# Hybrid attention on one Trainium2 core: scaling on GpSimd, outputs on ScalarE, and scores on the two row halves of the array

## The reference, cut to what matters

```
for each head h, branch b, tile t of 128 queries:
    s    = q[t, h] . k_b[keys up to the tile's end]^T / sqrt(64) + bias_b
    p    = exp(s - max s);   sum = p.sum() (+ exp(sink - max s) for "ban")
    fac  = 1 / sum, times gate_b[t, h] for the three branches of the first mixer
    y[t] += (p * fac) . v_b
```

## Time and profile before

| | us |
|---|---|
| median of 3 runs | 3504.17 (3500.81 to 3507.8) |
| the profiled execution, its own time | 3509.27 |
| its span in the profile | 3507.5 |
| busy in the span: PE, DVE, ACT, POOL | 2892.5, 1526.5, 452.8, 886.6 |
| mean granted TensorE clock | 0.903 of full |

### The profile page before, as it was taken

The page is one execution under the profiler, slowest core; times in us unless marked ns, Lnnn a source line. Parts: engine busy times, 40 slices in busy tenths (PEclk is TensorE's granted clock), DMA queues, the critical chain, the costliest instruction groups (busy, mean ns, idle before and its releaser), DMA issues.

```text
span 3507.5 us, 25672 instructions
## 1 busy us (share of the span) xinstructions
PE 2892.5 (82%) x9302; PEld 1717.2 (49%) x9302; DVE 1526.5 (44%) x2316; ACT 452.8 (13%) x1020; POOL 886.6 (25%) x633
## 2 busy tenths in 40 slices
PE   5999887989999999999997899477776666666666
PEld 3444656478888884444456647133332222222222
DVE  5664364122210000001016704765666667767765
ACT  1000232011011010001005501000010001100000
POOL 2111100000000000000000002554556566666663
PEclk9999878999999999999988999798897887888788
DMA  9999420356544443444640045999999999999998
GB/s 380 395 401 341 124 83 15 120 197 222 201 147 155 155 148 140 155 150 137 218 136 1 2 145 218 418 384 417 379 401 422 422 421 422 408 422 422 422 421 355
DMA packets 232373, 922.71 MB, mean 263 GB/s; under 512 B 17819, under 2 KB 37475, under 8 KB 160355
## 3 DMA queue, kind: packets, MB, share of 16 engines
q0 software_dynamic: 99840, 637.57, 44.3%
q1 hardware_dynamic: 132181, 283.96, 23.8%
q10 hardware_dynamic: 272, 0.13, 0.0%
HBM read 918.41 MB, written 8.44 MB: 264 GB/s over the span
## 4 chain that ended last, share of the span: by engine, by line
PE 55%; DMA 25%; DVE 11%; POOL 4%; issue 2%; ACT 2%; DVEq 0%; POOLq 0%; SPq 0%; ACTq 0%
PE ps L1219 17%; PE ps L907 11%; DMA arena<-in_peer_v,proj 10%; PE ps L1245 9%; PE ps L1444 6%; DMA proj<-in_peer_v,proj 4%; DMA proj<-in_peer_u,proj 4%; DMA ring<-in_w_in 3%; DMA arena<-in_w_mod 3%; PE ps L1028 3%; POOL arena L487 3%; PE ps L1421 2%; DVE proj L2049 1%; POOL proj L487 1%; DVE arena L2049 1%
## 5 line engine op out<-in xcount | busy, mean ns | idle before, releaser
L1444 PE MATMUL ps<-proj,gates 128*128 128x512 f32 x992 | 576.0, 745 | 394.2 <-DMA proj<-in_peer_v,proj 272.2
L1219 PE MATMUL ps<-hT,ring 128*128 128x256 f32 x2816 | 608.2, 379 | 1.5 <-ACT hT L526 1.5
L1444 PEld LDWEIGHTS ps<-proj,gates 128*128 128x128 f32 x992 | 233.3, 243 | 733.6 <-issue 604.3
L1219 PEld LDWEIGHTS ps<-hT,ring 128*128 128x128 f32 x2816 | 535.0, 190 | 74.9 <-issue 2.2
L487 POOL DMA_INDIRECT proj<-in_peer_u,proj x128 | 204.8, 1600 | 1427.6 <-DVE proj L2042 1265.1
L907 PE MATMUL ps<-ring,hT 128*128 128x512 f32 (+2 forms) x960 | 381.7, 558 | 8.7 <-DMA ring<-in_w_in 8.7
L2049 DVE CUSTOM_DVE_ANT_0 arena<-arena,yT 128x2048 f32<-128x2048 f32 x128 | 291.5, 2291 | 211.4 <-DMA arena<-in_peer_u,proj 210.9
L2049 DVE CUSTOM_DVE_ANT_0 proj<-proj,yT 128x2048 f32<-128x2048 f32 x128 | 292.1, 2291 | 126.8 <-DMA proj<-in_peer_u,proj 122.7
L1245 PE MATMUL ps<-ring,arena 128*128 128x512 f32 x704 | 304.1, 595 | 2.7 <-ACT arena L725 2.7
L907 PEld LDWEIGHTS ps<-ring,hT 128*128 128x128 f32 x960 | 175.6, 194 | 214.5 <-issue 192.6
L1444 PE MATMUL ps<-arena,gates 128*128 128x512 f32 x512 | 237.3, 607 | 35.9 <-DMA arena<-in_peer_v,proj 35.7
(11 more groups left out here) (410 smaller groups left out, 2568.3 us busy)
## 6 DMA issues: line engine op xcount, KB each, us to landing
arena<-in_w_mod POOLq DMA_DIRECT2D x96, 1024.0 KB, 12.4
ring<-in_w_in SPq DMA_DIRECT2D x52, 1024.0 KB, 12.1
ring<-in_ffn_w_gate SPq DMA_DIRECT2D x44, 1024.0 KB, 5.2
ring<-in_ffn_w_up SPq DMA_DIRECT2D x44, 1024.0 KB, 5.2
ring<-in_ffn_w_down SPq DMA_DIRECT2D x44, 1024.0 KB, 4.8
ring<-in_w_out SPq DMA_DIRECT2D x32, 1024.0 KB, 5.2
ring<-in_peer_wq SPq DMA_DIRECT2D x16, 1024.0 KB, 10.9
ring<-in_w_in SPq DMA_DIRECT2D x16, 960.0 KB, 18.2
```

The costliest lines, as they stand in the source:

```text
L1219: ins = pe.matmul(ps[:, 4 * m + f, 0:T], ring[:, s, k, P * f:P * (f + 1)], hT[:, KS * s + k, :], start=(s == 0 and k == 0), stop=(s == SLO ...
L1444: ins = pe.matmul(ps[:, 4 * t + b, :], diag[:, j, :], row_slots[n % ROWS][:, NB * b:NB * (b + 1)], start=(h == 0 and j == 0), stop=(h == H ...
```

## The change

What goes to which engine changes, and the order on PE:

- The multiplication of a unit by its factors goes from DVE to POOL (`scaled`). DVE signals `att_fac` when the factors are there; POOL waits for it and signals `att_p`. `q_in` goes to POOL too, behind `scaled(0)` of each pair, and the very first ahead of all pairs.
- `attended` goes from DVE to ACT, behind `turned_out(0)` and `turned_out(1)` of the next pair.
- `hyb["q"]` keeps both heads of a pair side by side in its two row halves, with two buffers that alternate by pair. It needs no zeros, so its memset goes, and `q_out` is two activations of 128 rows instead of four of 64.
- `score` is one head: a matmul of 64 rows, head 0 on the upper and head 1 on the lower row half. `half_scores(u, 0)` issues head 0 of unit u and head 1 of unit u + 1, `half_scores(u, 1)` the two others; between them PE waits until the first two have ended, as one bank would otherwise be written from both halves. PE does this at odd u only, for units u + 3 and u + 4, the first half ahead of `turn_p(u)` and the second behind it.
- All eight pairs are straight code on PE; ACT's loop takes two pairs a turn.

```diff
@@ GpSimd @@
+        def scaled(i, past, u):
+            t, br = UNITS[u]
+            n = {"cmp": (7, 15)[t]}.get(br, P * (t + 1))
+            pool_eng.wait_ge(*at("att_fac", at_unit(i, past, u + 1)))
+            p = hyb["p"][:, u % 4, :, 0:n]
+            pool_eng.tensor_tensor(p, p, hst["sum"][:, u, :].unsqueeze(2).to_broadcast([P, 2, n]), ALU.mult).then_inc(sem("att_p"), 1)
+        def head_pair(i, past, more=True):
+            for u in range(NU):
+                scaled(i, past, u)
+                if u == 0 and more:
+                    pool_eng.wait_ge(*(at("att_turned", at_unit(i, past, -3)) if past else at("q_turned", 1)))
+                    q_in(i, past + 1)
+        pool_eng.wait_ge(*at("kv_twice", 1))
+        q_in(0, 0)
...
@@ ScalarE @@
-        def q_out(k):
-            for h in range(2):
-                r = slice(DK * h, DK * (h + 1))
-                ins = act.activation(hyb["q"][r, k, h, :], ps[r, 4 + k, T:2 * T], ACT.Copy, scale=DK ** -0.5)
-            ins.then_inc(sem("q_out"), 1)
+        def q_out(pair, k):
+            act.activation(hyb["q"][:, pair % 2, k, :], ps[:, 4 + k, T:2 * T], ACT.Copy, scale=DK ** -0.5).then_inc(sem("q_out"), 1)
...
+        def attended(i, past, k, u):
+            act.wait_ge(*at("att_pv", at_unit(i, past, u + 2)))
+            act.copy(yT[:, bass.ds(i + (past + 8 * k), 1), :], ps[:, 6 + k, 0:T].unsqueeze(1)).then_inc(sem("att_out"), 1)
...
                 turned_out(i, past, u, more)
+                if u < 2 and past:
+                    attended(i, past - 1, u, NU - 2 + u)
...
@@ TensorE @@
-        def score(i, past, u):
+        def score(i, past, u, h, second):
...
+            r = slice(DK * h, DK * (h + 1))
+            ins = pe.matmul(ps[:, u % 4, T * h:T * h + n], hyb["q"][r, (past + u // NU) % 2, int(br == "ban"), P * t:P * (t + 1)], keys[r], start=True, stop=True)
+            if second:
+                ins.then_inc(sem("att_score"), 1)
+            return ins
+        def half_scores(i, past, u, n):
+            for v, h in (((u, 0), (u + 1, 1)), ((u, 1), (u + 1, 0)))[n]:
+                ins = score(i, past, v, h, n)
+            return ins
...
             for u in range(NU):
-                if u + 4 < NU or more:
-                    score(i, past, u + 4)
+                ahead = u % 2 and (u + 3 < NU or more)
+                if ahead:
+                    half_scores(i, past, u + 3, 0).then_inc(sem("first_half"), 1)
                 turn_p(i, past, u, more)
+                if ahead:
+                    pe.wait_ge(*at("first_half", i * 4 + (4 * past + u // 2 + 3)))
+                    half_scores(i, past, u + 3, 1)
                 if u:
                     values(i, past, u - 1)
...
@@ VectorE @@
-        link(vec.memset(hyb["q"], 0.0), "q_zero")
...
-                link(vec.tensor_tensor(s, s, gate, ALU.mult))
-            p = hyb["p"][:, u % 4, :, 0:n]
-            link(vec.tensor_tensor(p, p, s.unsqueeze(2).to_broadcast([P, 2, n]), ALU.mult), "att_p", wait=False)
+                link(vec.reciprocal(s, s))
+                link(vec.tensor_tensor(s, s, gate, ALU.mult), "att_fac", wait=False)
...
                 weigh(i, past, u)
                 if u + 3 < NU or more:
                     row_max(i, past, u + 3)
-                if u == 0 and more:
-                    vec.wait_ge(*(at("att_turned", at_unit(i, past, -3)) if past else at("q_turned", 1)))
-                    q_in(i, past + 1)
-                if u == 1 and past:
-                    attended(i, past - 1, 1, NU - 1)
-            attended(i, past, 0, NU - 2)
```

More of the change, by code:

```diff
@@ L483, in _, with q_in @@
                 pool_eng.dma_start(mod["late"][:, j % 4], w_mod[:, 2 * j:2 * j + 2, (10 + n) * MB:(11 + n) * MB]).then_inc(sem(f"mod_slot{j % 4}"), 16)
+        def q_in(i, past):
+            for k, col in enumerate((QA, QB)):
+                ins = pool_eng.tensor_copy(hyb["q_in"][:, k], p2[:, :, bass.ds(i * P + (col + P * past), P)])
+            ins.then_inc(sem("q_in"), 1)
+        def scaled(i, past, u):
[12 more added lines that the diff above has]
+        q_in(0, 0)
+        head_pair(0, 0)
+        with pool_eng.Fori(0, 6) as i:
+            head_pair(i, 1)
+        head_pair(0, 7, False)
         def gather(table, g, r, n):
@@ L770, in turned_out @@
             if more and u in (2, 3):
-                q_out(u - 2)
+                q_out(past + 1, u - 2)
             if past or u >= 2:
@@ L775, in turned_out @@
             act.copy(hyb["pT"][0:r, u % 2, 0:n, :], ps[0:r, 4 + u % 2, 0:P * n].rearrange("p (a b) -> p a b", b=P)).then_inc(sem("att_pT"), 1)
-        act.wait_ge(*at("q_zero", 1))
         act.wait_ge(*at("q_turned", 1))
         for k in range(2):
-            q_out(k)
+            q_out(0, k)
         for u in range(2):
             softmax_exp(0, 0, u)
+        def attended(i, past, k, u):
+            act.wait_ge(*at("att_pv", at_unit(i, past, u + 2)))
+            act.copy(yT[:, bass.ds(i + (past + 8 * k), 1), :], ps[:, 6 + k, 0:T].unsqueeze(1)).then_inc(sem("att_out"), 1)
         def head_pair(i, past, more=True):
@@ L789, in head_pair @@
                 turned_out(i, past, u, more)
+                if u < 2 and past:
+                    attended(i, past - 1, u, NU - 2 + u)
         head_pair(0, 0)
-        with act.Fori(0, 6) as i:
+        with act.Fori(0, 6, 2) as i:
             head_pair(i, 1)
+            head_pair(i, 2)
         head_pair(0, 7, False)
+        for k in range(2):
+            attended(0, 7, k, NU - 2 + k)
         act.wait_ge(*at("att_out", 17))
@@ L1287, in _ @@
         pe.wait_ge(*at("kv_out", 1))
-        def score(i, past, u):
+        def score(i, past, u, h, second):
             t, br = UNITS[u % NU]
             g = kv_head(past, u)
-            if past or u >= 4:
+            if not second and (past or u >= 4):
                 pe.wait_ge(*at("att_exp", at_unit(i, past, u - 2)))
-            if u in (NU, NU + 3):
+            if not second and u in (NU, NU + 3):
                 pe.wait_ge(*at("q_out", i * 2 + (2 * past + 3 + u // (NU + 3))))
[L1297 to L1306, removed]
+            if br == "cmp":
+                n = (7, 15)[t]
+                keys = hyb["kc"][:, g, 0:n]
+            else:
+                n = P * (t + 1)
+                keys = hyb["kT"][:, 2 * ("slc", "win", "ban").index(br) + g, 0:n]
+            r = slice(DK * h, DK * (h + 1))
[7 more added lines that the diff above has]
+            return ins
         def turn_q(k):
@@ L1366, in _ @@
         pe.wait_ge(*at("q_out", 2))
[L1367 to L1376, removed]
+        for u in (0, 2):
+            half_scores(0, 0, u, 0).then_inc(sem("first_half"), 1)
+            pe.wait_ge(*at("first_half", u // 2 + 1))
+            half_scores(0, 0, u, 1)
+        for pair in range(8):
+            head_pair(0, pair, pair < 7)
         values(0, 7, NU - 1)
@@ L1892, in _ @@
             vec.memset(stat[:, 17 + k:18 + k], 0.0).then_inc(sem(name), 1)
-        link.n["att_out"] = 1
         vec.wait_ge(*at("evac_act", EVB["out2"] + 2))
@@ L1901, in _ @@
         vec.memset(hyb["v"], 0.0)
-        vec.memset(hyb["v_cmp"], 0.0)
-        link(vec.memset(hyb["q"], 0.0), "q_zero")
+        link(vec.memset(hyb["v_cmp"], 0.0))
         for kind in range(3):
@@ L1947, in weigh @@
             t, br = UNITS[u]
-            n = {"cmp": (7, 15)[t]}.get(br, P * (t + 1))
             vec.wait_ge(*at("att_exp", at_unit(i, past, u + 2)))
@@ L1952, in weigh @@
                 link(vec.tensor_tensor(s, s, hst["esink"][:, u, :], ALU.add))
-            link(vec.reciprocal(s, s))
-            if br != "ban":
+                link(vec.reciprocal(s, s), "att_fac", wait=False)
+            else:
                 gate = hst["gate"][:, 3 * t + ("cmp", "slc", "win").index(br), bass.ds(i * 2 + 2 * past, 2)]
-                link(vec.tensor_tensor(s, s, gate, ALU.mult))
-            p = hyb["p"][:, u % 4, :, 0:n]
-            link(vec.tensor_tensor(p, p, s.unsqueeze(2).to_broadcast([P, 2, n]), ALU.mult), "att_p", wait=False)
+                link(vec.reciprocal(s, s))
+                link(vec.tensor_tensor(s, s, gate, ALU.mult), "att_fac", wait=False)
         nb = UNITS.count((0, "ban")) + UNITS.count((1, "ban"))
[L1961 to L1968, removed]
         def head_pair(i, past, more=True):
@@ L1974, in head_pair @@
                     row_max(i, past, u + 3)
-                if u == 0 and more:
-                    vec.wait_ge(*(at("att_turned", at_unit(i, past, -3)) if past else at("q_turned", 1)))
-                    q_in(i, past + 1)
-                if u == 1 and past:
-                    attended(i, past - 1, 1, NU - 1)
-            attended(i, past, 0, NU - 2)
         vec.wait_ge(*at("bias_in", 16))
-        q_in(0, 0)
         for u in range(3):
@@ L1987, in _ @@
         with vec.Fori(0, 6) as i:
-            link.begin(i, vec_chain=NU + 2 * nb + NU + nb + (NU - nb), att_max=NU, att_p=NU, q_in=1, att_out=2)
```

(2 more changed lines are left out.)

## The result

The changed kernel takes 3543.2 us in the median (3540.0 to 3548.1, 4 runs) against 3505.9 for the kernel before in the same session: a ratio of 1.0110, 95% interval 1.0092 to 1.0128. It is slower by 37 us; the forecast was 28 us (3532, range 3512 to 3555). The profiled execution took 3546.0 us with a span of 3544.2.

The account below looks back on a forecast made before the run. DVE was taken to set the turn. Six loop turns 4.05 us longer gave +24.3, pair 0 +3.7, pair 7 +2.1, the start -2.6: together +27.5 us, forecast 3532 us, range 3512 to 3555.

Parts of the forecast that it names:

- the round: At odd steps DVE's next row maximum waits for POOL's scaling, PE's transposes and a score: 8.00 us more a turn.
- the first rival: TensorE's clock falls in the turns: 2.1 us a turn in the rounds, +16, 3548 us; chance 0.20.
- What bounds the kernel: Loop turns of 19.67 us: no engine is full, and DVE, working in order, sets the turn.
- The length of the rounds: Steps 1, 3, 5, 7, from last factor instruction to next row maximum: 2.55, 2.30, 2.94, 2.89, together 10.68 us.
- The change of shape: On PE, idle weight loading ahead of the 64-row scores: 0.17 us a round, bounds 0 and 0.35.
- The turn: A loop turn: 8.00 us more for rounds against 3.95 that DVE gives up, so 4.05 longer, 23.7 us.
- the two cmp multiplications: Multiplications of the two cmp units, leaving DVE in each turn; their saving was not counted.
- PE is waiting then anyway: PE's scores may overlap on the row halves, but half a unit's score time is worth nothing beyond the round.
- Beside it: Other engines in a turn: ACT stays near 11.5 us busy, POOL some 8 of 23.7; both covered.
- Faster: Rival: rounds don't hold DVE, a turn about 15 us, 3469 us; needs rounds below 6.6; chance 0.05.
- Balance: Rival: handovers and change of shape cost almost nothing, 2.2 to 2.6 us less a turn, 3512 us; 0.08 for within 0.2%.
- The shared port: Rival: POOL's query copies hold DVE's small SBUF instructions in step 0, up to 0.72 us a turn, 3537; chance 0.10.

Follow-up runs that it names:

- e9: Kernel before with the POOL and ACT moves, 128-row scores of units u+3 and u+4 at odd u behind the transposes: 3535.7 us, ratio 1.0095.
- e10: Kernel before with the POOL and ACT moves, 128-row scores of units u+3 and u+4 at odd u ahead of the transposes: 3477.9 us, ratio 0.9932.
- e2: Changed kernel with the two score halves issued at even u for units u+4 and u+5, still round the transposes: 3473.9 us, ratio 0.9914.
- e7: Changed kernel plus two unread 128x256 matmuls at every even unit, ahead of PE's wait for the scaled unit: 3516.8 us, ratio 1.0038.
- e8: e2 with the second half of the scores right behind the first, both ahead of the transposes: 3465.4 us, ratio 0.9895.
- e11: e9 plus two unread 128x256 matmuls at every even unit, ahead of PE's wait for the scaled unit: 3523.8 us, ratio 1.0063.

## Why the prediction was right, and what was mis-sized

The mechanism of the round was right. That the total came so near was luck: two errors of opposite sign partly cancel, and the first rival, the falling clock with its 3548, was 5 us off, nearer than the forecast's 11.

- **What bounds the kernel, and the round.** Right, and shown by e9 against e10 and e2 against after. The four waits stand at the odd units, over 1 us each.
- **The length of the rounds** was too large: 10.68 against 9.19 in e7. DVE to POOL took 0.08 instead of 0.15; POOL 0.61 and 1.04 instead of 0.72 and 1.08; in step 5 the score and what follows it took 0.49 + 0.18 instead of 0.40 + 0.36. The change of shape, 0.17 by the earlier trace rows, showed as 0.09 in step 5 (0.56 for four transposes instead of 0.47).
- **The turn.** The sum gave 23.7 at full clock; it was 21.8. The shorter rounds explain 1.5 of the 1.9 us. The rest I didn't trace; the two cmp multiplications that I hadn't counted may be part of it.
- **The clock** is the step that failed. I had it as a rival with a chance of 0.20 and 2.1 us a turn, on the ground that turns with 5 us of gaps had stood at full clock. It fell to 0.59 and 0.75 and costs 3.5 us a turn (e7). The price was too low because I charged only the transposes and scores in the round. "PE is waiting then anyway" doesn't hold at low clock: in step 1 the values and the first half end 1.4 us after POOL is done, and that round takes 4.27 us instead of 2.20 at full clock.
- **The total.** The two errors are -1.9 and +3.5 us a turn. Measured +37 us against +28.
- **Beside it.** ACT's 11.2 us and the absence of any wait of DVE for `attended` were right. POOL is busy for 6.1 us a turn, not 8. From the keys' copies to the first score it is 25.6 us (1821.67 to 1847.25) instead of 28.7 (1824.21 to 1852.94): 3.1 us earlier, where 2.6 was forecast.
- **The rivals.** Faster falls: the rounds sum to 9.19, not under 6.6. Balance falls as a time, but of the 2.2 to 2.6 us a turn that it took off the forecast 1.9 came true at full clock (21.8 instead of 23.7); the clock hid it. The shared port shows, and is small: in each of the six loop turns DVE's L1977 (the old L1940) takes 0.24 to 0.26 us beside POOL's query copies and ends with them (1925.82 + 0.24, where the copies end at 1926.05), and 0.16 in pair 7, which has no copies, as in all 16 cases before. That is 0.08 to 0.10 us a turn at most, against the 0.72 allowed. Row halves that don't run beside each other, for which the sum left room, are ruled out by e2's 0.63 against 0.86. The Trainium skill, "TensorEngine Tiling (Array Packing)", Key Properties, says that a change of mode drains the array. e8 agrees in kind: it has half as many changes and is 0.3 us a turn faster than e2, though no row shows a drain by itself.

## What to carry to other kernels

When work is moved to a free engine, read what the next instruction of the engine that sets the pace waits for: here the moves were worth 1.3%, and a score issued one step later, behind the transposes, turned them into a loss of 1% (e9; 1.1% with the row halves), part of it through a lower clock (e7, e11). A lead that is counted in units has to be recounted when two units are grouped. And before the array is split by rows, ask whether PE is the bound, whether the matmuls are wide enough, and what the shorter work does to the clock.

## What the runs showed of the hardware

- Work added to PE made the kernel 26 us faster: two 128x256 matmuls at every even unit, with 18.3 us of PE busy in 21.8, brought the granted clock to 1.00 (0.92 in one of five turns), where after had 0.59 and 0.75 with 18.9 to 23.3 us busy (at the lower clock the same matmuls count longer). With 128-row scores and 18.8 us busy in 24.1 it was 0.75, and without such gaps, 13.7 in 14.1, 1.00; but before had 1.00 with 14.5 in 19.7.
- Two 64-row matmuls of 256 columns on the two row halves take 0.63 us to the next start, two of 128 rows 0.86; with 128 columns it was 0.42 against 0.45, and with the wait between the halves 0.97 against 0.81 for 7 and 128 columns together.
- POOL multiplies 128x512 by a broadcast factor in 1.04 us and 128x256 in 0.61, DVE in 0.69 and 0.43; a handover from DVE to POOL took 0.08 us.
- A small DVE instruction on two SBUF operands (L1977) took 0.24 to 0.26 us instead of 0.16 when POOL's copies ran beside it, and ended with them.
